# Up projection of a streaming encoder's MLP by Strassen's seven block products, 12 tile pairs a layer, in four chunks of 1024 features

## The reference

```python
def _layer(x, l, p, k_past, v_past, conv_buf, h0):
    ...
    x = x + _rms(m @ p['w_out'], p['g_mix_post'])
    f = jnp.square(jax.nn.relu(_rms(x, p['g_mlp_pre']) @ p['w_up'])) @ p['w_down']
    x = x + _rms(f, p['g_mlp_post'])
    return x, k_rows, v, conv_new, h_last
```

## Time and profile before

| | us |
|---|---|
| median of three runs | 2022.09 |
| the three runs | 2022.09, 2027.35, 2021.73 |
| span of the profiled execution, first to last instruction | 2018.6 |
| TensorE busy | 1975.9 (98%) |
| VectorE busy | 1072.3 (53%) |
| ScalarE busy | 955.6 (47%) |
| GpSimd busy | 279.1 (14%) |

### The profile page before, as it was taken

The page is one execution under the profiler, slowest core; times in us unless marked ns, Lnnn a source line. Parts: engine busy times, 40 slices in busy tenths (PEclk is TensorE's granted clock), DMA queues, the critical chain, the costliest instruction groups (busy, mean ns, idle before and its releaser), DMA issues.

```text
span 2018.6 us, 38666 instructions
## 1 busy us (share of the span) xinstructions
PE 1975.9 (98%) x15630; PEld 1929.2 (96%) x15630; DVE 1072.3 (53%) x1986; ACT 955.6 (47%) x1503; POOL 279.1 (14%) x306
## 2 busy tenths in 40 slices
PE   7999999999999999999989999999999999999997
PEld 7999999999998999999989999999999999999997
DVE  6657575765437432333467676767644464224334
ACT  5466666565236431342365757565732554213333
POOL 4312121100101200120041212120001012002100
PEclk9999999999999999999999999999999999999999
DMA  5323232322332323232323232322223323233331
GB/s 136 107 60 105 63 100 69 83 71 78 93 95 70 87 84 93 84 94 84 98 60 98 64 100 72 99 76 75 74 84 94 95 65 92 84 92 86 90 88 67
DMA packets 308455, 172.00 MB, mean 85 GB/s; under 512 B 7592, under 2 KB 303872, under 8 KB 308320
## 3 DMA queue, kind: packets, MB, share of 16 engines
q1 hardware_dynamic: 300768, 155.47, 27.0%
q0 software_dynamic: 7520, 14.59, 2.6%
q10 hardware_dynamic: 32, 0.04, 0.0%
HBM read 158.86 MB, written 11.21 MB: 84 GB/s over the span
## 4 chain that ended last, share of the span: by engine, by line
PE 81%; ACT 9%; DVE 6%; issue 3%; DMA 1%; SPq 0%; ACTq 0%; DVEq 0%
PE PJ L698 65%; PE PJ L710 3%; PE PJ L880 3%; PE PX L908 2%; ACT w_hi L1136 2%; PE PX L926 1%; DVE w_lo L1611 1%; PE PX L946 1%; DVE T L1722 1%; PE PX L962 1%; PE PX L710 1%; DMA w_raw<-in_w_in 1%; DVE uc L1855 1%; ACT L1353 1%; DVE Y L1643 1%
## 5 line engine op out<-in xcount | busy, mean ns | idle before, releaser
L1611 DVE TENSOR_TENSOR w_lo<-w_raw,w_hi 128x1024 fp32r<-128x1024 f32 x284 | 384.2, 1356 | 371.5 <-ACT w_hi L1136 370.4
L698 PE MATMUL PJ<-h_hi,w_hi 128*128 128x272 f32 x2304 | 489.9, 294 | 2.6 <-DVE T L1722 1.9
L698 PE MATMUL PJ<-h_hi,w_lo 128*128 128x272 f32 x2304 | 474.8, 288 | 0.0
L698 PE MATMUL PJ<-h_lo,w_hi 128*128 128x272 f32 x2304 | 473.8, 287 | 0.0
L1136 ACT ACTIVATE w_hi<-w_raw 128x1024 fp32r<-128x1024 f32 x284 | 297.6, 1051 | 233.4 <-DMA w_raw<-in_w_down 116.9
L698 PEld LDWEIGHTS PJ<-h_hi,w_hi 128*128 128x128 f32 x2304 | 359.3, 189 | 12.8 <-issue 9.5
L698 PEld LDWEIGHTS PJ<-h_lo,w_hi 128*128 128x128 f32 x2304 | 360.7, 188 | 0.0
L698 PEld LDWEIGHTS PJ<-h_hi,w_lo 128*128 128x128 f32 x2304 | 359.5, 189 | 0.0
L698 PE MATMUL PJ<-u_hi,w_hi 128*128 128x272 f32 x960 | 198.4, 288 | 0.0
L698 PE MATMUL PJ<-u_hi,w_lo 128*128 128x272 f32 x960 | 197.4, 288 | 0.0
L698 PE MATMUL PJ<-u_lo,w_hi 128*128 128x272 f32 x960 | 197.1, 287 | 0.0
(11 more groups left out here) (351 smaller groups left out, 3595.4 us busy)
## 6 DMA issues: line engine op xcount, KB each, us to landing
w_raw<-in_w_in SPq DMA_DIRECT2D x110, 512.0 KB, 3.8
w_raw<-in_w_down SPq DMA_DIRECT2D x64, 512.0 KB, 3.8
w_raw<-in_w_up SPq DMA_DIRECT2D x62, 512.0 KB, 4.1
w_raw<-in_w_branch_attn SPq DMA_DIRECT2D x16, 512.0 KB, 3.8
w_raw<-in_w_branch_lru SPq DMA_DIRECT2D x16, 512.0 KB, 3.8
w_raw<-in_w_out SPq DMA_DIRECT2D x16, 512.0 KB, 3.8
out_prompt_k<-stage POOLq DMA_DIRECT2D x16, 256.0 KB, 2.8
out_prompt_v<-GA POOLq DMA_DIRECT2D x8, 512.0 KB, 4.5
```

Of the source, the lines that this page charges most:

```text
L698: mm = pe.matmul(PJ[:, buf, half, 0:HT], w[a], src[b][:, k0 + k, HT * half:HT * half + HT], start=first and k == 0 and a + b == 0, stop=en ...
L1611: dve.tensor_tensor(low(n)[:], raw(n), w_hi[:, n.hi, :, :].bitcast(F32), ALU.subtract).then_inc(w_lo_ready, 1)
```

## The change

The up projection's first chunk (eight tiles) stays as it is. The other 24 up tiles of a layer are taken as 12 pairs. A pair is a 2 x 2 block matrix: its two output tiles by the two halves of the contraction (k-tiles 0 to 3 and 4 to 7). The activation is one too: the same two halves of the contraction by the two halves of the tokens. Seven products of four k-tiles by 272 tokens (12 matmuls each) replace eight.

- Activation blocks (`mix`): four sums of blocks of h, made once a layer. GpSimd first multiplies `X` by the gain into `h_full` in four instructions of 4 x 272 elements (`full_h`) and later makes the third sum; VectorE makes the other three (`make_mix`) behind `h_full`; ScalarE and VectorE split them (`split_mix`, `mix_rest`).
- Weight blocks (`part`): seven a pair, three of them raw halves of the tiles and four of them sums: two by GpSimd (`sum_13`), two by VectorE (`sum_24`). Each is rounded by ScalarE (`split_part`) and its rest is written by VectorE (`part_rest`), 128 x 512 elements each. While TensorE works on pair g, they are made for pair g + 1.
- Products: PSUM banks 0 to 3 of `PX`. Product 0 is copied away by ScalarE (`first_product`) so that product 4 can go on in its bank; VectorE combines the banks with the help of `w_mix` into the two relu inputs `T`, and ScalarE takes over the relu, then squares and rounds as before. GpSimd writes `u_lo`.
- Chunks: four of 1024 features, so each down output tile is one weight tile (48 matmuls), added to `Y` three times instead of once. The last two output tiles are both taken by token halves (`down_end`).
- All loops of the MLP are written out.

In the code (`...` marks what is left out):

```diff
+            def full_h(l, k, h):
+                kk, cc = quarter(k, h)
+                pool.tensor_tensor(h_full[:, kk, cc], X[:, kk, cc], par[:, kk, 16 * l + R_MPRE:16 * l + R_MPRE + 1].broadcast_to([P, 4, HT]),
+                                   ALU.mult).then_inc(h_full_ready, 1)
...
+            def sum_13(l, c, q):
+                g, n, n1 = pair_no(l, c, q), mlp_tile(l, c, 2 * q), mlp_tile(l, c, 2 * q + 1)
...
+                    pool.wait_ge(part_done, 6 * (g - 1) + 2)
+                pool.tensor_tensor(part_f[1][:], w1[:, 0:4, :], w1[:, 4:8, :], ALU.add).then_inc(sum13_ready, 1)
...
+                pool.tensor_tensor(part_f[3][:], w[:, 0:4, :], w1[:, 0:4, :], ALU.add).then_inc(sum13_ready, 1)
...
+                pool.wait_ge(x_new, x_count(2 * l + 1) + 5)
+                full_h(l, 0, 0)
+                full_h(l, 1, 0)
+                pool.wait_ge(x_new, x_whole(2 * l + 1))
+                full_h(l, 0, 1)
+                full_h(l, 1, 1)
+                u_rest(l, 0, 0, 0)
+                u_rest(l, 0, 1, 1)
...
+                for c in range(1, 4):
+                    sum_13(l, c, 0)
+                    for q in range(4):
+                        if q < 3:
+                            sum_13(l, c, q + 1)
+                        u_rest(l, c, 2 * q + 1, 2 * q)
+                        u_rest(l, c, 2 * q, 2 * q + 1)
```

TensorE's `fast_pair`, what each product waits for beside its weights:

```diff
+                for f in range(7):
+                    o = PX[:, (0, 1, 2, 3, 0, 3, 1)[f], 0:HT]
...
+                    if f == 0:
...
+                        need(pe, product_kept, g)
+                    if f == 1:
+                        pe.wait_ge(evacuated, n.value)
+                    if f == 4:
+                        pe.wait_ge(first_kept, g + 1)
+                    if f == 5:
+                        pe.wait_ge(crossed, 4 * g + 2)
+                    if f == 6:
+                        pe.wait_ge(crossed, 4 * g + 3)
```

ScalarE's `fast_pair`:

```diff
+                act.activation(first_product[:], PX[:, 0, 0:HT], ACT.Copy).then_inc(first_kept, 1)
+                if q < 3:
+                    for f in range(4):
+                        split_part(l, c, q + 1, f)
...
+                act.activation(T[:, 0, 0:HT], PX[:, 0, 0:HT], ACT.Relu).then_inc(product_kept, 1)
+                if q < 3:
+                    split_part(l, c, q + 1, 4)
+                act.wait_ge(crossed, 4 * g + 4)
+                u_square(l, c, 2 * q, 2 * q + 1, slice(0, NT))
+                if q < 3:
+                    split_part(l, c, q + 1, 5)
+                    split_part(l, c, q + 1, 6)
+                act.wait_ge(evacuated, n.value + 2)
+                u_square(l, c, 2 * q + 1, 2 * q, slice(HT, NT))
```

VectorE's first chunk:

```diff
+                for i in range(8):
+                    up_plain(l, i)
+                    if i == 0:
+                        make_mix(l)
+                    if i > 3:
+                        mix_rest(l, i - 4)
```

More of the change, by code:

```diff
@@ L181, in hybrid_encoder @@
         Y = at("Y", [P, KT, NT], F32, V_AT)
+        h_full = at("h_full", [P, KT, NT], F32, V_AT)
         s1 = at("s1", [P, 1792], F32, S_AT)
@@ L963, in weigh_v @@
                 mm.then_inc(pv_done, 1)
[L965 to L979, removed]
@@ L981, in down_end, with down_first @@
-            def down_end(l):
[L983 to L987, removed]
+            U = (u_hi, u_lo)
+            def down_first(l, c):
+                n = mlp_tile(l, c, 8)
+                tile_in(n)
+                pe.wait_ge(evacuated, n.value - (2 if c else 1))
+                order = (0, 1, 2, 3, 4, 5, 7, 6) if c else range(KT)
+                for at_, k in enumerate(order):
+                    if at_ % 2 == 0 and k < 6:
+                        pe.wait_ge(u_lo_ready, 32 * l + 8 * c + k + 2)
+                    elif at_ > 5:
+                        pe.wait_ge(u_lo_ready, 32 * l + 8 * c + at_ + 1)
+                    w = (w_hi[:, n.hi, k, :], low(n)[:, k, :])
+                    for a, b in ((0, 0), (0, 1), (1, 0)):
+                        for half in range(2):
+                            mm = pe.matmul(PJ[:, 0, half, 0:HT], w[a], U[b][:, k, HT * half:HT * half + HT],
+                                           start=at_ == 0 and a + b == 0, stop=at_ == KT - 1 and a == 1)
+                mm.then_inc(tile_done, 1)
@@ new lines, in down @@
+            def down(l, c, m):
+                n = mlp_tile(l, c, 8 + m)
+                if m < 6:
+                    split_lo(mlp_tile(l, c, 10 + m))
+                elif c < 3:
+                    if m == 6:
+                        sum_24(l, c + 1, 0)
+                    for f in ((0, 1), (2, 3))[m - 6]:
+                        part_rest(l, c + 1, 0, f)
+                dve.wait_ge(tile_done, n.value + 1)
+                y, o = halves(Y[:, m, :]), proj(n)
+                if c == 0:
+                    dve.tensor_copy(y, o).then_inc(evacuated, 1)
+                    return
+                dve.tensor_tensor(y, y, o, ALU.add).then_inc(evacuated, 1)
+                if c == 3:
+                    dve.wait_ge(evacuated, n.value + 1)
+                    if m == 0:
+                        dve.wait_ge(x_rs, 6 * l + 6)
+                    dve.tensor_tensor(Y[:, m, :], Y[:, m, :], r2q[:], ALU.mult).then_inc(f_scaled, 1)
+                    if m > 1:
+                        y_sum(l, 1, m - 1)
```

504 lines of the change are left out of this document (324 added, 180 removed).

## The result

| | before | after |
|---|---|---|
| median of the runs, us | 2023.51 (4 runs, 2021.73 to 2027.35) | 2111.61 (4 runs, 2109.02 to 2112.67) |
| ratio, 95% interval | | 1.044 (1.0427 to 1.0452) |
| span of the profiled execution, us | 2018.6 | 2110.8 |

The account below looks back on a forecast made before the run. The prediction took TensorE, busy 98%, as the bound. To the 2018.6 us span it added 51.4 for pairs, 21.8 renewal, 1.0 layer's end and 5 clock: 2097.8, plus 3.5 for the runs' median, 2101 us, range 2060 to 2135.

Parts of the forecast that it names:

- The saving: Pairs: 84 matmuls replace 96, 1.49 us less each, 35.8 us over 24 pairs if TensorE never waits.
- The pair: Middle pairs: a circle of waits through the engines' lists takes 15.7 us against TensorE's 10.45; six chunks add 51.4 us.
- VectorE stands behind GpSimd: Pairs and renewal: two-input SBUF instructions of VectorE stand while GpSimd reads, after 0.13 us of start-up; 2.3 us a circle.
- The renewal: Ahead of the MLP: `full_h` delays VectorE's `h_lo`, then `make_mix` and `u_lo` delay the third tile's relu; +21.8 us.
- The layer's end: Layer's end: one more half tile in `renew`, some 0.4 us of VectorE and ScalarE a layer; +1.0 us.
- The clock: Pairs: TensorE's granted clock falls after waits, 0.3 us a pair; +5 us, too small if low clock covers over 40.
- The rest at nothing: MLP: extra additions to `Y`, the activation's split and weight loads stay covered by TensorE's work and cost nothing.
- Faster: Rival: the pair's circle closes within 10.45 us, TensorE stays the bound, 1987 us; gain needs under 11.94; chance 0.07.
- The lists alone: Rival: VectorE rarely stands behind GpSimd, pairs cost +12.6 us, renewal 0, 2036 us; chance 0.06.
- The clock* (2126 and more): Rival: the clock falls in most pairs, costing 1.7 us in each of 18; 2126, up to 2140 us; chance 0.10.
- Half of it: Rival: pairs as worked out but `full_h` costs the renewal nothing, 2079 us; with both halved, 2065; chance 0.16.
- not what it says: Rival: compiled order shows seven products and all waits, but something cancels the effect, no change; chance 0.03.

Follow-up runs that it names:

- all_lists: Changed kernel with both_orders, mix_spread and end_only together, and in a chunk's last pair the first down tile's split behind the second `w_mix`: 1996.11 us, ratio 0.9869.
- gpsimd_writes_only: Changed kernel with GpSimd's two weight sums and `u_lo` in the pairs replaced by memsets that read nothing (results wrong): 2054.27 us, ratio 1.0156.
- vector_order: Changed kernel with only VectorE's list in a pair reordered, results ahead of preparation for the next pair, same work: 2049.0 us, ratio 1.014.
- end_only: Changed kernel with only the layer's end reordered: next layer's second weight-tile split behind the last squares, sum of squares inside the half tile: 2105.94 us, ratio 1.0415.
- four_chunks_only: Changed kernel without pairs and mixes: all up tiles whole, in four chunks, with the changed layer's end: 2029.64 us, ratio 1.0039.
- late_full_h: Changed kernel with GpSimd's four `full_h` behind the last `h_lo` and `make_mix` moved from the third tile's relu: 2098.8 us, ratio 1.0385.
- mix_spread: Changed kernel with `full_h` late, all mix sums by VectorE, one in each of up tiles 4 to 7, splits in down tiles: 2090.15 us, ratio 1.0333.
- both_orders: Changed kernel with VectorE's and ScalarE's lists in a pair both reordered, same work: 2027.7 us, ratio 1.0021.

## Why the prediction was right, point by point

- **The saving** (1.49 us a pair). Right in size, shown by all_lists: 32.9 of 35.8 us.
- **The pair** (15.7 us, a stage of four 14.5 us of waits, +51.4). Last `T` to last `T` took 15.2 to 16.2 us in the twelve middle pairs, 15.82 in the mean; the waits were where they were put, 62.4 us for 87 forecast. A stage cost 57.3 us in the mean for 56.4, 57.0 more in all for 51.4 and the clock's 5. The 87 was too high because the waits were counted at TensorE's full clock: 1.0 and 2.3 us in the pair at 853.07 for 2.6 and 2.66, since at the low clock its own work fills the rest. The low clock covered 44 us of the pairs; half of that is 22 us of longer work, and with 62.4 of waits it makes 84.
- **VectorE stands behind GpSimd.** Right, and shown by gpsimd_writes_only. The 0.13 us of start-up beside the other engine was right too: the `part_rest` at 860.13 ended 0.54 after GpSimd for 0.69 of work, so 0.15 of it was done before. `part_rest` has a mean of 0.822 and 0.943 and `sum_24` of 0.957 and 0.905, for near 0.85. The forecast also cites the Trainium skill for a full block of the loser ("SBUF — State Buffer", "Who interferes with whom"), which would have given about 2127: that section calls the shared port an exclusive lock, but writes the full block of VectorE's two-port modes. The row at 860.13 does not show a full block; what the sum is short by lies elsewhere (below).
- **The renewal** (+21.8). 18.6. The mechanism was right: VectorE late behind `full_h`, then the relu of the third tile late behind `make_mix`. The sizes were not, and partly made up for each other: `h_full` takes 2.15 us, not 2.7 (twice the price of 544 elements), in the first layer `h_lo` cost TensorE 1.6 us more of waits in the first token half for 2.7 forecast and 1.2 in the second for 5.2, and the relu's wait was 4.2 for 3.0. That is 7.1 us; with half of the 4.2 us at the low clock it is the stage's 9.3 a layer, for 10.9. The granted clock fell here too:

```profile
630.00:635.00 5.00, 5.00 (x31) 5.00 (x30) 4.90 (x11) 1.17 (x3) 0.33 (x1) 0.75 0.00 0
```

  (stretch 630 to 635 us after the change, columns as in the earlier trace rows, where the window with these numbers had 1.00 before): the granted clock is 0.75 in the mean of the stretch, 1.2 GHz for half of it, behind a wait of 3.58 us. In this stage it cost nothing. The renewal takes 51.6 us a layer in all five kernels with the early `full_h`, whether the low clock covers 4.2 us of it with 7.1 of waits for `h_lo` or 6.9 us with 5.5 (vector_order and end_only, first layer): VectorE sets its length.
- **The layer's end** (+1.0). This step failed: 6.8 us. "One more half tile in `renew`" counted the instructions, but not that VectorE's addition of tile 7's first half stands behind a weight split that waits for ScalarE. end_only shows 2.8 of it as order; four_chunks_only, without pairs, has 5.8 of it; the cause of the other 4 is open.
- **The clock** (+5). About right in size for the pairs, for which it was made, and too small for the kernel. "More than 40 us" at the low clock was to mean that; it covered 96 us (25 before). In the pairs, 44 of these: each of the 12 middle pairs had one stretch of 3.4 us at 1.2 GHz and took 15.82 in the mean; the only two middle pairs without one, in late_full_h and end_only, took 15.45 and 15.44. That would be 0.4 a pair, an estimate that rests on two pairs, while those with a stretch scatter from 15.2 to 16.4 over the kernels. With one last pair of 11.50 for 9.98 it makes 6 us. There the low clock falls into time in which TensorE would have waited. Outside the pairs the forecast had no term for it, and it cost 5.6 us in the up tiles 4 to 7: TensorE waited for nothing there and still took 26.7 us a layer for 23.9, with 6 us of it at 1.2 GHz behind the wait of 4.2. In vector_order the low clock covered 3.3 us of the same tiles and they took 25.5; in mix_spread none, and they took 24.0.
- **The rest at nothing.** Right: additions to `Y`, weight loads and chunks cost nothing (four_chunks_only), no product of a pair waited for a DMA.
- **Rivals.** *Faster* needed a circle under 11.94; it is there in both_orders (10.56), not in the change. *The lists alone* (2036) fell with the standing. *The clock* (2126 and more) fell: a low stretch costs a middle pair about 0.4 us, not 1.7. *Half of it* (2079, 2065) fell with the renewal's 18.6 us, and *not what it says* with the slower kernel.

The sum, 92.2 for 79.2 in the span, is short by 13: 5.8 the end, 5.6 the clock behind the renewal, 0.6 the pairs with their clock, 4.1 the scatter of the rest, and 3.2 back from the renewal. Mechanism and size are right for the pairs, which are most of it. Of the other terms the renewal was put too high and the end and the clock too low; that they leave only about 8 us together is in part luck. One sign failed: TensorE's busy time was to fall by some 36 us and rose by 7.4, since the low clock makes its records longer.

## What to carry to other kernels

An engine at 59% can bound one at 94% if its list puts preparation ahead of results: add up the circle from the last result of one step to the last of the next, through every list it passes, and compare it with the bound's own work; then put each result where its product is done and the preparation behind it. The same instructions took 15.8 or 10.6 us a pair. When work is added to a stretch in which an engine is full, move it to one where it has room, and look at the whole stage, since much of what is gained in one place can return in the next (6.3 of 15.0 us in late_full_h).

## What the runs showed of the hardware beyond that

- GpSimd stands behind VectorE as VectorE does behind GpSimd. Its subtraction of 1088 elements took 3.53 us from 652.26, while VectorE's third mix ran until 653.45, and VectorE's next addition (653.37, 3.00 us for 0.72) ended 0.59 after it. Without the stand some 2.4 us are left, an estimate from these times, near the 2.15 of `full_h` for as many elements. In the second layer a `u_lo` beside VectorE's mixes took 2.42 us for 1.36.
- In the changed kernel the granted clock fell once in every middle pair, beside a wait of 2.1 to 2.9 us; but other waits of 2.31 us (those that ended at 780.46 and 869.49) brought no fall. In the pairs of gpsimd_writes_only (18 waits, up to 1.6 us) and of vector_order (24 waits, up to 1.2 us) it stayed at 1.00. The first of these works on zeros, the second on the kernel's own data.
